# Split weights of a one-core decoder block: high parts in three 1 MB places, one expert row loaded early, the first matrix by columns, one bias matmul moved

## The reference

```
proj  = rms_norm(x) @ w_in                      # 1024 x 4608
y1    = conv branch: a * sigmoid(g), causal depthwise conv of 31 taps over 512 channels,
        layer norm, silu, @ w_conv_out
y2    = attention of 8 heads (q, k normed, ALiBi), @ w_attn_out
h     = x + (sigmoid(g1) * y1 + sigmoid(g2) * y2) @ w_out
u2    = rms_norm(h);  logits = u2 @ w_router + b_router;  top 4 of 32 experts per token, softmax gates
out   = h + sum over chosen e: gate * (clamped_swiglu(u2 @ w_up_gate[e] + b_up_gate[e]) @ w_down[e] + b_down[e])
```

## Time and profile before

| | us |
|---|---|
| median of 3 runs | 1081.63 (1079.66 to 1081.91) |
| the profiled execution | 1083.46 |
| its span | 1081.7 |
| PE busy | 895.0 (83%) |
| DVE busy | 440.4 (41%) |
| ACT busy | 253.8 (23%) |
| HBM read | 431.59 MB, 400 GB/s over the span |

### The profile page before, as it was taken

How to read it: one execution, slowest core, us unless ns; L and a number is a source line. 1 busy time by engine, 2 the same in 40 slices (tenths; PEclk the granted TensorE clock), 3 DMA queues, 4 the chain that set the end, 5 groups by cost and what they waited for, 6 DMA issues and landing times.

```text
span 1081.7 us, 18596 instructions
## 1 busy us (share of the span) xinstructions
PE 895.0 (83%) x6874; PEld 407.3 (38%) x6875; DVE 440.4 (41%) x1111; ACT 253.8 (23%) x410; POOL 5.5 (1%) x35
## 2 busy tenths in 40 slices
PE   9999999996666769599956899978996956996666
PEld 8789996332112223133311333322331311332221
DVE  6898986432222114244422344431442312443222
ACT  5568753121111002122211122220121201212111
POOL 2000000000000000000000000000000000000000
PEclk9999999998888789899998999997998987999889
DMA  9763599999999999999999999999999999999996
GB/s 329 264 194 128 224 384 422 412 434 431 429 435 430 431 429 436 431 430 430 436 431 429 434 431 431 429 436 430 431 430 436 431 429 434 431 431 429 436 421 277
DMA packets 32982, 432.96 MB, mean 400 GB/s; under 512 B 3013, under 2 KB 3425, under 8 KB 18112
## 3 DMA queue, kind: packets, MB, share of 16 engines
q1 hardware_dynamic: 32432, 431.99, 94.7%
q10 hardware_dynamic: 528, 0.66, 0.2%
HBM read 431.59 MB, written 1.05 MB: 400 GB/s over the span
## 4 chain that ended last, share of the span: by engine, by line
PE 58%; DMA 31%; another core or an unknown queue 5%; SPq 3%; DVE 2%; issue 0%; ACT 0%; ACTq 0%; DVEq 0%
PE bank L1559 22%; PE bank L1596 11%; DMA down_odd<-in_w_down 10%; PE bank L1254 9%; DMA down_even<-in_w_down 8%; DMA up_even<-in_w_up_gate 8%; DMA up_odd<-in_w_up_gate 4%; PE bank L1494 3%; PE bank L1541 3%; PE bank L1473 3%; PE bank L1192 3%; SPq L498 2%; SPq L502 1%; DMA down_odd<-in_w_in 1%; DVE up_odd L836 1%
## 5 line engine op out<-in xcount | busy, mean ns | idle before, releaser
L1559 PE MATMUL bank<-up_even,reg_r 128*32 128x512 f32 x1472 | 195.4, 687 | 80.3 <-DMA up_even<-in_w_up_gate 80.3
L1559 PE MATMUL bank<-up_odd,reg_r 128*32 128x512 f32 x1408 | 183.1, 673 | 74.3 <-DMA up_odd<-in_w_up_gate 74.3
L1148 DVE SCALAR_TENSOR_TENSOR ys<-bank,gslot,ys 64x512 fp32r<-64x512 f32 x90 | 67.4, 749 | 228.3 <-ACT ys L758 226.9
L758 ACT ACTIVATE ys<-bank,gslot 64x512 fp32r<-64x512 f32 x90 | 61.5, 683 | 315.2 <-PE bank L1596 314.1
L1559 PEld LDWEIGHTS bank<-up_even,reg_r 128*32 128x32 f32 x1472 | 51.2, 124 | 220.2 <-issue 132.1
L1559 PEld LDWEIGHTS bank<-up_odd,reg_r 128*32 128x32 f32 x1408 | 49.5, 122 | 204.7 <-issue 120.7
L752 ACT ACTIVATE reg_m<-reg_m 128x256 f32<-128x256 f32 x45 | 18.8, 418 | 429.6 <-DVE reg_m L1127 429.6
L1596 PE MATMUL bank<-down_odd,reg_r 128*32 128x512 f32 x704 | 81.7, 595 | 15.2 <-DMA down_odd<-in_w_down 15.2
L1596 PE MATMUL bank<-down_even,reg_r 128*32 128x512 f32 x736 | 83.7, 595 | 6.1 <-DMA down_even<-in_w_down 6.1
L1127 DVE TENSOR_SCALAR reg_m<-bank 128x256 f32<-128x256 f32 x45 | 19.1, 424 | 168.1 <-PE bank L1559 168.1
L752 ACT ACT_TABLE_LOAD x45 | 57.7, 1283 | 3.4 <-issue 2.5
(11 more groups left out here) (277 smaller groups left out, 1015.4 us busy)
## 6 DMA issues: line engine op xcount, KB each, us to landing
up_odd<-in_w_up_gate SPq DMA_DIRECT2D x29, 4096.0 KB, 46.5
up_even<-in_w_up_gate SPq DMA_DIRECT2D x28, 4096.0 KB, 39.7
down_even<-in_w_down SPq DMA_DIRECT2D x15, 4096.0 KB, 42.4
down_odd<-in_w_down SPq DMA_DIRECT2D x14, 4096.0 KB, 47.1
down_even<-in_w_in SPq DMA_DIRECT2D x16, 1024.0 KB, 5.2
up_even<-in_w_up_gate SPq DMA_DIRECT2D x5, 2048.0 KB, 14.0
up_odd<-in_w_up_gate SPq DMA_DIRECT2D x3, 2048.0 KB, 12.5
up_odd<-in_w_up_gate SPq DMA_DIRECT2D x6, 1024.0 KB, 47.4
```

Of the source, the lines that this page charges most:

```text
L758: nc.scalar.activation(ys[0:64, half, :], YB[r, :], ACT.Identity, scale=gslot[r, :]).then_inc(y_high, 1)
L1148: nc.vector.scalar_tensor_tensor(ys[64:P, half, :], YB[r, :], gslot[0:64, :], ys[0:64, half, :].bitcast(F32), ALU.mult, ALU.subtract).then ...
L1559: ins = mm(UP[q * SLOTS:(q + 1) * SLOTS, :], XT[:, k, :], up_columns(a, k, q), start=False, stop=(k == KD - 1), skip_group_check=True)
```

## The change

The high parts get three places of 1 MB, used in turn by the halves: (i, b) lies in place (2i + b - 2) % 3, the split half of group 0 in the third. So ACT may split a half only once PE is through with the half three before it, and this is now asked for in every group. The fourth row of `up_even`, row 3, is free after that, and SP loads expert 0's row 3 right behind rows 6 and 7, and rows 0 to 2 at the end of the dense part, with one place fewer released.

Group 0 is loaded by columns: first the 256 columns of the plain product in four pieces by pairs of k, then the other 256 in one load with a semaphore of its own. PE's transposes of the parameters stand ahead of the second bank of group 1. The second half of group 2 is split on ACT behind both sigmoids (before: ahead of them) and on DVE behind the first taps of the first two channel blocks. The taps are dealt out differently among the `weights_low` calls: 3 taps for each pair of channel blocks at first (before: 5), and between the halves of groups 3 to 5 then 2, 2, 2 and 5 taps (before: 1 ahead of group 3, then 1, 2, 1 and 4). In the last expert every tile puts its own bias in front of its up product; none stands behind the last down product any more.

```diff
--- before.py
+++ after.py
@@ -99,7 +99,7 @@
             return nc.alloc_sbuf_tensor_at(name, [P, n], F32R, offset=at + 4 * column)
 
         w_lo = [part("w_lo0", E_AT, 0, 4096), part("w_lo1", DOWN_AT, 0, 4096), part("w_lo2", DOWN_AT, 4096, 4096)]
-        w_hi = [part("w_hi0", EVEN_AT, 0, 4096), part("w_hi1", EVEN_AT, 4096, 4096)]
+        w_hi = [part(f"w_hi{j}", EVEN_AT, 2048 * j, 2048) for j in range(3)]
 
 
         u_r = [part(n, EVEN_AT, 8192 + 2048 * i, 2048)[:, :].rearrange("p (k t) -> p k t", k=KD)
@@ -232,6 +232,7 @@
             return [sem(n) for n in names.split()]
 
 
+        g0_rest = sem("g0_rest")
         par_in, g1_in, small_in, bup_in, bdown_in, out_sem = sems("par_in g1_in small_in bup_in bdown_in out_sem")
         x_in = [sem(f"x_in{m}") for m in range(MT)]
         half_in = [[sem(f"half_in{s}_{b}") for b in range(2)] for s in range(2)]
@@ -297,17 +298,15 @@
         def place(i):
             return 1 + (i - 1) % 2 if i else 0
 
-        def w_whole(i):
-            return [t.rearrange("p (k n) -> p k n", k=KD) for t in (w_hi[i % 2][:, :], w_lo[place(i)][:, :], slots[place(i)])]
-
         def w_half(i, b):
-            return [t[:, 2048 * b:2048 * b + 2048].rearrange("p (k n) -> p k n", k=4)
-                    for t in (w_hi[i % 2], w_lo[place(i)], slots[place(i)])]
+            return [w_hi[(2 * i + b - 2) % 3][:, :].rearrange("p (k n) -> p k n", k=4)] + [
+                t[:, 2048 * b:2048 * b + 2048].rearrange("p (k n) -> p k n", k=4) for t in (w_lo[place(i)], slots[place(i)])]
+
+        first_low, first_whole = [t.rearrange("p (k n) -> p k n", k=KD) for t in (w_lo[0][:, :], slots[0])]
+        first_split = [w_hi[2][:, :].rearrange("p (k n) -> p k n", k=KD), first_low[:, :, 256:512], first_whole[:, :, 256:512]]
 
         def w_split(i, b):
-            if i == 0:
-                return [t[:, :, 256 * b:256 * b + 256] for t in w_whole(i)]
-            return w_half(i, b)
+            return first_split if i == 0 else w_half(i, b)
 
         def arrived(eng, i, b):
             eng.wait_ge(half_in[(i - 1) % 2][b], 16 * ((i + 1) // 2))
@@ -402,9 +401,10 @@
                 sp.dma_start(brt[:], b_router.partition_broadcast(P)).then_inc(small_in, 16)
                 sp.dma_start(wr[:], w_router.rearrange("(p k) n -> p k n", k=KD)).then_inc(small_in, 16)
 
-            first = w_whole(0)[2]
+            first = first_whole
             for c in range(4):
-                sp.dma_start(first[:, 2 * c:2 * c + 2, :], win[:, 2 * c:2 * c + 2, 0:512]).then_inc(g0_in[c], 16)
+                sp.dma_start(first[:, 2 * c:2 * c + 2, 0:256], win[:, 2 * c:2 * c + 2, 0:256]).then_inc(g0_in[c], 16)
+            sp.dma_start(first[:, :, 256:512], win[:, :, 256:512]).then_inc(g0_rest, 16)
             for i in (1, 2):
                 for b in range(2):
                     load_half(i, b)
@@ -412,6 +412,7 @@
             used(sp, 0)
             load_down(1, 2, 4, 1)
             load_up(0, 3, 0)
+            load_up_rows(0, 3, 4, 0)
             for i in range(3, CONV_W):
                 for b in range(2):
                     load_half(i, b)
@@ -438,13 +439,14 @@
             load_up_rows(1, 0, 1, 1)
             for b in range(2):
                 half_used(sp, OUT_W, b)
-                load_up_rows(0, 2 + b, 3 + b, 0)
+                if b == 1:
+                    load_up_rows(0, 0, 1, 0)
                 load_down(0, b, 1 + b, 0)
             half_used(sp, OUT_W + 1, 0)
-            load_up_rows(0, 0, 1, 0)
+            load_up_rows(0, 1, 2, 0)
             load_down(0, 2, 3, 0)
             used(sp, OUT_W + 1)
-            load_up_rows(0, 1, 2, 0)
+            load_up_rows(0, 2, 3, 0)
             load_up(0, 2, 0)
             load_down(0, 3, 4, 0)
             sp.wait_ge(parts_full, MT)
@@ -589,12 +591,11 @@
 
             def weights_high(i, b):
                 if i == 0:
-                    for c in range(4):
-                        act.wait_ge(g0_in[c], 16)
+                    act.wait_ge(g0_rest, 16)
                 else:
                     arrived(act, i, b)
-                if 2 <= i < ATT_W:
-                    half_used(act, i - 2, b)
+                if i >= 2:
+                    half_used(act, *((i - 2, 1) if b == 0 else (i - 1, 0)))
                 hi, _, w = w_split(i, b)
                 nc.scalar.activation(hi, w, ACT.Identity).then_inc(w_hi_ready, 1)
 
@@ -609,14 +610,14 @@
             full(act, U_G + 1)
             nc.scalar.activation(aT[:, 2:4, :], bank[(U_G + 1) % 4][:].rearrange("p (a b) -> p a b", a=2),
                                  ACT.Identity).then_inc(bank_free[(U_G + 1) % 4], 1)
-            for b in range(2):
-                weights_high(2, b)
+            weights_high(2, 0)
 
             for b in range(2):
                 u = U_G + 2 + b
                 full(act, u)
                 nc.scalar.activation(sq[:, 2 * b:2 * b + 2, :], bank[u % 4][:].rearrange("p (a b) -> p a b", a=2),
                                      ACT.Sigmoid).then_inc(bank_free[u % 4], 1)
+            weights_high(2, 1)
             for b in range(2):
                 weights_high(3, b)
 
@@ -815,8 +816,7 @@
                                     rstd_c.unsqueeze(1).to_broadcast([P, 2, T]), ALU.mult).then_inc(bank_free[U_G % 4], 1)
             for b in range(2):
                 weights_low(1, b)
-            for b in range(2):
-                weights_low(2, b)
+            weights_low(2, 0)
             dve.wait_ge(par_full, 1)
             nc.vector.tensor_copy(par[:, 0:28], PAR_BANK[:, 0:28]).then_inc(par_ready, 1)
             nc.vector.tensor_scalar(par[:, 28:29], PAR_BANK[:, 28:29], HD ** -0.5, None, ALU.mult).then_inc(par_ready, 1)
@@ -846,18 +846,19 @@
                 nc.vector.tensor_tensor(hp[:, 2 * b:2 * b + 2, TAPS - 1:], aT[:, 2 * b:2 * b + 2, :],
                                         sq[:, 2 * b:2 * b + 2, :], ALU.mult).then_inc(a_ready, 1)
                 dve.wait_ge(a_ready, b + 1)
-                taps(0, 5, (2 * b, 2 * b + 1))
+                taps(0, 3, (2 * b, 2 * b + 1))
+                if b == 0:
+                    weights_low(2, 1)
 
             early_taps = 16
-            taps(5, 6)
             weights_low(3, 0)
-            taps(6, 7)
+            taps(3, 5)
             weights_low(3, 1)
+            taps(5, 7)
+            weights_low(4, 0)
             taps(7, 9)
-            weights_low(4, 0)
-            taps(9, 10)
             weights_low(4, 1)
-            taps(10, 14)
+            taps(9, 14)
             for b in range(2):
                 weights_low(5, b)
 
@@ -1206,24 +1207,24 @@
                 return ins
 
             def first_group_bank(low):
-                w = w_whole(0)
+                w = first_split
                 u = group_use(0, 1)
                 pe.wait_ge(w_hi_ready, 1)
                 pe.wait_ge(u_hi_ready, 2)
                 claim(u)
                 for c in range(2):
-                    ins = product3_by_part(bank[u % 4][:, c * T:(c + 1) * T], lambda a, k: w[a][:, k, (2 + c) * P:(3 + c) * P],
+                    ins = product3_by_part(bank[u % 4][:, c * T:(c + 1) * T], lambda a, k: w[a][:, k, c * P:(c + 1) * P],
                                            lambda a, k: u_r[a][:, k, :], KD, low)
                 ins.then_inc(bank_full[u % 4], 1)
 
             def channel_group_bank(i, b, before=None):
                 split(i, b)
-                w = w_whole(i)
+                w = [w_half(i, 0), w_half(i, 1)]
                 u = group_use(i, b)
                 claim(u)
                 for c in range(2):
                     ch = 2 * b + c
-                    ins = product3(bank[u % 4][:, c * T:(c + 1) * T], lambda a, k: w[a][:, k, ch * P:(ch + 1) * P],
+                    ins = product3(bank[u % 4][:, c * T:(c + 1) * T], lambda a, k: w[k // 4][a][:, k % 4, ch * P:(ch + 1) * P],
                                    lambda a, k: u_r[a][:, k, :], KD, before=before if c == 0 else None)
                 ins.then_inc(bank_full[u % 4], 1)
 
@@ -1234,19 +1235,19 @@
                     if c == 0 and k % 2 == 0:
                         freed(pe, U_XT + k // 2)
                         pe.wait_ge(g0_in[k // 2], 16)
-                    ins = mm(bank[U_G % 4][:, c * T:(c + 1) * T], w_whole(0)[2][:, k, c * P:(c + 1) * P], xg[:, k, :],
+                    ins = mm(bank[U_G % 4][:, c * T:(c + 1) * T], first_whole[:, k, c * P:(c + 1) * P], xg[:, k, :],
                              start=(k == 0), stop=(k == KD - 1))
                     if c == 0 and k == 3:
                         rstd_broadcast()
             ins.then_inc(bank_full[U_G % 4], 1)
             first_group_bank(lambda k: pe.wait_ge(u_lo_ready, k // 4 + 1))
             channel_group_bank(1, 0, lambda k: split(1, k // 4))
-            channel_group_bank(1, 1)
             pe.wait_ge(par_in, 16 * 8)
             nc.tensor.transpose(PAR_BANK[:, 0:30], rows, ident[0:30, 0:30])
             for c in range(KC):
```

(7 more changed lines are left out.)

## The result

The changed kernel takes 1083.01 us (median of 20 runs, 1081.88 to 1085.44), the one before 1081.69 in the 20 runs taken beside them. The ratio is 1.0016, its 95% interval 1.0009 to 1.0023: slower by 1.0 to 2.5 us, 1.3 between the medians. The forecast was 1080.0 with a range up to 1082.6. The change is within 0.2% of no change, but on the other side of it, and outside the range.

The account below looks back on a forecast made before the run. The expert part was taken as bound by its loaded bytes, the dense part by PE almost everywhere. Row -2.44, places and taps +0.9, columns +0.25 and last bias -0.3 gave -1.6: 1080.0 from 1081.63, range 1077.4 to 1082.6.

Parts of the forecast that it names:

- The places and the taps: Dense part to group 5: DVE's idle time moves, PE starts group 5 0.7 earlier but loses 1.6 to clock: +0.9.
- The early row: Load queue: row 3 moves from the dense part's end to about 23 us, saving 2.44 if the queue stays fed.
- the sign that I had named as wrong: Among the signs against the forecast: a load queue that idles near 178 us, at the end of the dense part.
- Rival B: Queue runs dry at 178 and the row saves nothing, or 1 KB pieces are slow: up to 1082.4, 12%.
- Rivals A and C: A: group 5's wait costs no clock or is shorter, 1078.1, 28%; C: `weights_high(6, 1)` delays scaled copies, 1084.1, 10%.
- Group 0 by columns: First loads: PE's plain product starts earlier, but 1 KB pieces load slower: +0.25, between -0.1 and +1.8.
- The last bias: Kernel's end: without PE's bias for a nonexistent tile the left store leaves earlier: -0.3, bounds 0 and -1.1.

Follow-up runs that it names:

- row late: The changed kernel with expert 0's row 3 loaded at the end of the dense part again, together with row 2, three places kept: 1084.77 us, 1.0031.
- row behind group 3: The changed kernel with row 3 issued behind the two halves of group 3 instead of ahead of them: 1082.00 us, 1.0005.
- both repairs with group 0 whole: The changed kernel with more taps ahead of `weights_low(2, 1)`, row 3 behind group 3's halves and group 0 loaded as before: 1076.77 us, 0.9954.
- release held: The kernel before with the parameter transposes early, and expert 0's row 2 held back from the first release to the last: 1078.92 us, 0.9976.
- columns: The kernel before with the parameter transposes early, plus group 0 loaded by columns: 1077.97 us, 0.9967.
- clock kept: The changed kernel with 24 extra matmuls of 256 columns, results unused, ahead of group 5's wait: 1081.81 us, 1.0002.
- early transposes: The kernel before with only the five parameter transposes moved ahead of the second bank of group 1: 1077.53 us, 0.9967.

## Why the prediction was wrong, point by point

Put together from the traces, the change is -2.44 for the row, +2.7 for places and taps, +1.4 for the releases, 0 for the columns and -0.4 for the last bias: +1.3, which is what the medians show. The prediction had -2.44, +0.9, no such term, +0.25 and -0.3.

That the sum closes to a tenth is partly luck. Made in the same way for the other eleven kernels, each with its own dense end, it comes out right for the row late and up to 1.5 us too fast elsewhere (row behind group 3: -0.6, measured +0.7; both repairs with group 0 whole: -5.9, measured -4.5). Dense ends from single traces scatter by up to 1 us with group 0's load, and the 1.4 is a difference of medians whose intervals overlap; the streams give it nearer 2. The terms are shown one by one, their sum only to 1 or 1.5 us.

**"The places and the taps", mis-sized: +0.9, and it was +2.7.** The mechanism held step by step: the transposes early, ACT's wait for group 1, DVE's 4.8 us of idle time, one long wait of PE at group 5, with 0.32 us left at group 3 where I had none, the clock at 0.50. The sentence that failed is that group 3's first half "lands near 40.0 instead of 39.36" and that "nothing is lost". It was split at 41.37, 1.4 later than that. Two things were wrong. I took the landing of rows 6 and 7 from the trace before, 34.8; it was 35.9, and row 3's 38.7 and not 37.2. And I compared the half's landing with "about 42", when DVE wants the high part, and forgot that ACT's split, 1.92, stands between. By my own numbers DVE reaches that low part at 44.6 - 2.24 = 42.4, so the half had to land by 40.4: the slack was 0.4 and not 2. DVE idled 1.16 us, so group 5 started at 71.91 and not at 70.7. The wait grew to 4.16, and with it the clock's price from the 1.6 taken to 2.3. Moving the row behind group 3 restored 70.67 and 1.6. Why rows 6 and 7 came late stays open. They landed at 35.3 to 36.5 in the eight traces with columns and at 34.8 to 35.5 in the five without (35.96 against 35.09 in the pair that differs by nothing else), so group 0's columns may have a part in it; no run took the columns out of the changed kernel itself. The start is shown to hang on the row's place; the clock's part less surely, as the kernel with the row late had 71.00 and 2.8. My upper bound for this term, +1.4, was half a microsecond of longer wait at the same clock price; it should have let the clock cost more than in the one trace I had.

**"The early row", right in its size, wrong in its check.** The row saved 2.2 us in two pairs of kernels by the medians (2.3 and 1.8 in the streams), near the 2.44. But I tested the queue at one point, the release at 178.04, and by landing times: 2.8 us of backlog less 2.44. By landing times that was right. The load issued at 180.77 landed 6.0 us later, 0.75 above the 5.25 of an empty queue. The engines were nevertheless at 315 and 332 GB/s there, and there were notches from 174 on. This was the sign that I had named as wrong, a queue that idles near 178, or close to it; row 3 landed after 38, and the first expert tile came 1.7 later, not 0.5 to 1.5. A backlog read off the last landing doesn't say that the engines are all fed.

**The missing term, +1.4.** I read the shifted releases in the diff and gave them no price. The kernel with four places and one release held shows it: 1.4 us between the medians, 2.1 in the stream. It belongs to the three places, not to the early row, since the changed kernel without the early row loses it too (1.8 us of stream from 165 to 185). Rival B had the place, a queue that runs dry near 178, but put it down to the row and bounded it by what the row saves. In truth the row paid and the rhythm cost, and B's upper time, 1082.4, is near the measured 1083.0 for a different reason.

**Rivals A and C did not happen.** The clock cost more than taken, not nothing. The scaled copies came in time: PE's 24 matmuls ahead of the first scores run from 81.86 to 84.72, and the scores follow at once; the copies ended at 84.43, with the 0.3 us of margin that I had worked out.

**Group 0 by columns.** No effect on the time beyond the scatter; +0.25 can't be told from 0. The estimate of the rate, 355 GB/s, was near the mean of 367 in eight traces with columns, against 395 in five without. The Trainium skill (DMA: Bandwidth & Descriptors, Specifications) puts line rate at pieces of 512 B and more. These means lie some 7% apart, so they don't bear out one rate for both sizes. In the two pairs of kernels that differ in the columns alone, no effect on the time is clear of the scatter.

**The last bias.** 0.4 us in the tail against 0.3 forecast, in single traces.

The range failed because the two errors have one sign: each new wait of the places was traced along ACT, DVE and PE, and not along SP, whose releases the same waits control.

## What to carry to other kernels

An in-order engine that must wait should have independent work ahead of the waiting instruction, not behind it. Moving twelve tap instructions of DVE was worth 6 us here, and moving five transposes of PE alone was worth 4. When a ring of buffers gets fewer places, list every release that shifts, on the loading queue too, and compare the bytes moved up to each point, not only the landing of the nearest load. A prefetch ahead of a load that compute is about to need costs the slack of that load, so put it one load further back.

## What the runs showed that was not expected

- **The clock's price isn't one number.** PE waits of 2.50 and 3.54 us cost 1.6 us each in the work behind them, the two longest, of 4.06 (row late) and 4.16 us (the changed kernel), cost 2.8 and 2.3. From 3.54 to the longest two the wait grew by 0.5 to 0.6 us, and wait and clock together by 1.7 and 1.3. The order of the last two says that the length of the wait alone doesn't set the price.
- **A short backlog doesn't keep the DMA engines full.** With landings 0.7 to 2.2 us later than on an empty queue, slices of 0.6 us fall to 144 to 223 GB/s, while the same queue holds 419 where they are 4 to 5 us later. That single engines run out while others still work would explain it. It fits that with the row late, while rows 6 and 7 are still landing near 34 us, slices show 26 GB/s, a sixteenth of 419; but no view shows the engines one by one, so it is argued and not shown.
- **The router's stage runs at either clock, whatever the kernel.** In five of the thirteen traces (before, row late, release held, columns, clock kept) it fell to 0.50, with no wait of PE over 0.4 us in that stage; in the others it stayed at 1.00. From the dense end to PE's first expert tile these five take 45.8 to 45.9 us and the others 44.8. Two kernels whose dense ends lie 0.13 us apart, early transposes and columns, fell on different sides. So the 1 us of the 2.7 that the changed kernel seems to win back there belongs to the execution and not to the change, and it doesn't reach the stream that sets the end.
